# A peer layer in one core: tile 0's experts chosen ahead of the dense tiles, and sixteen instead of eleven row groups inside the first gates

## The reference, cut to what matters

```python
def peer(h, w_query, sub_keys, expert_down, expert_up):   # 512 tokens, 8 heads, 128 x 128 experts
    qry = (ht @ w_query).reshape(T, PEER_HEADS, 2, PEER_HALF_2)
    sub_scores = jnp.einsum('thpc,hpkc->thpk', qry, sub_keys)
    top_s, top_i = lax.top_k(sub_scores, K)                # K = 16, for each half of the key
    cand_s = top_s[:, :, 0, :, None] + top_s[:, :, 1, None, :]
    cand_id = top_i[:, :, 0, :, None] * N_KEYS + top_i[:, :, 1, None, :]
    best_s, best_c = lax.top_k(cand_s.reshape(T, PEER_HEADS, K * K), K)
    expert_id = jnp.take_along_axis(cand_id.reshape(...), best_c, axis=-1)
    gate = jax.nn.softmax(best_s, axis=-1)
    u = expert_down[ids]                                   # 128 rows of 1024 for each token
    act = jax.nn.gelu(jnp.einsum('pd,ped->pe', x, u)) * gate
    return jnp.einsum('pe,ped->pd', act, expert_up[ids])
```

## Time and profile before

| | us |
|---|---|
| median of three runs (lowest, highest) | 3564.9 (3564.6, 3565.7) |
| the profiled execution | 3564.92 |
| its span | 3563.0 |
| TensorE busy | 3195.5 (90%) |
| VectorE busy | 2433.8 (68%) |
| ScalarE busy | 1317.7 (37%) |
| gate loop from, to the first weighed block, first peer layer | 748.8, 886.1 |
| first weighed block, end of the last second product, first layer | 886.1, 1824.5 |
| the same in the second layer | 2615.6, 3554.9 |

### The profile page before, as it was taken

The page is one execution under the profiler, slowest core; times in us unless marked ns, Lnnn a source line. Parts: engine busy times, 40 slices in busy tenths (PEclk is TensorE's granted clock), DMA queues, the critical chain, the costliest instruction groups (busy, mean ns, idle before and its releaser), DMA issues. The chain is left out here.

```text
span 3563.0 us, 45086 instructions
## 1 busy us (share of the span) xinstructions
PE 3195.5 (90%) x16120; PEld 1998.7 (56%) x16120; DVE 2433.8 (68%) x5465; ACT 1317.7 (37%) x3292; POOL 1329.9 (37%) x1028
## 2 busy tenths in 40 slices
PE   6988889945999999999979998996589999999989
PEld 3443554534666666666534465454456666666654
DVE  1037752789897987877761234359989799788777
ACT  2122211134765655541011125112456556555300
POOL 0000000016565676766610000000556566676665
PEclk9999889967999999999989998998689999999999
DMA  3213213128999999999962110211689999999998
GB/s 119 81 61 138 99 65 130 44 76 313 345 405 349 402 398 405 409 409 409 409 251 71 53 65 13 105 49 48 245 311 386 381 374 391 405 409 409 409 409 346
DMA packets 271695, 908.11 MB, mean 255 GB/s; under 512 B 30536, under 2 KB 31192, under 8 KB 270960
## 3 DMA queue, kind: packets, MB, share of 16 engines
q0 software_dynamic: 147456, 536.94, 38.7%
q1 hardware_dynamic: 124016, 368.29, 27.4%
HBM read 900.90 MB, written 4.22 MB: 254 GB/s over the span
## 5 line engine op out<-in xcount | busy, mean ns | idle before, releaser
L679 PE MATMUL psum<-hT,mod 128*128 128x256 f32 x4096 | 986.8, 396 | 74.6 <-ACT hT L1094 41.5
L679 PEld LDWEIGHTS psum<-hT,mod 128*128 128x128 f32 x4096 | 793.4, 198 | 203.8 <-issue 96.0
L1104 ACT ACTIVATE levels<-key_numbers,hT 128x128 bf16<-128x128 f32 x1712 | 542.6, 388 | 367.4 <-PE psum L715 361.1
L1864 POOL DMA_INDIRECT w<-in_peer_u,tmp x172 | 234.9, 1366 | 895.7 <-DVEq L1551 789.3
L1693 DVE SCALAR_TENSOR_TENSOR tmp<-w,small,tmp 128x1024 f32<-128x1024 f32 x339 | 435.6, 1285 | 63.8 <-DMA w<-in_peer_up,tmp 27.0
L1673 DVE CUSTOM_DVE_ANT_0 w<-w,hn 128x1024 f32<-128x1024 f32 x342 | 407.8, 1222 | 65.5 <-DMA w<-in_peer_down,tmp 32.1
L1864 POOL DMA_INDIRECT big<-in_peer_down,tmp x86 | 119.0, 1383 | 769.1 <-DVEq L1551 711.7
L715 PEld LDWEIGHTS psum<-x,levels 128*128 128x128 bf16 x6144 | 226.8, 102 | 258.5 <-DVE levels L1613 128.3
L715 PE MATMUL psum<-x,levels 128*128 128x32 bf16 x6144 | 240.9, 196 | 141.2 <-DVE levels L1613 119.4
L689 PE MATMUL psum<-rows,big 128*128 128x512 f32 x800 | 358.6, 592 | 0.0
L1864 POOL DMA_INDIRECT w<-in_peer_down,tmp x170 | 233.0, 1370 | 114.4 <-DVE small L1673 71.4
(11 more groups left out here) (300 smaller groups left out, 4049.7 us busy)
## 6 DMA issues: line engine op xcount, KB each, us to landing
mod<-in_uT SPq DMA_DIRECT2D x256, 512.0 KB, 6.8
rows<-in_peer_v SPq DMA_DIRECT2D x64, 512.0 KB, 6.8
rows<-in_peer_up SPq DMA_DIRECT2D x64, 512.0 KB, 6.8
w<-in_w_in SPq DMA_DIRECT2D x14, 2048.0 KB, 7.8
w<-in_ada_w SPq DMA_DIRECT2D x12, 2048.0 KB, 7.9
srow<-in_peer_v SPq DMA_DIRECT2D x32, 512.0 KB, 7.0
tmp<-in_peer_v SPq DMA_DIRECT2D x32, 512.0 KB, 6.9
srow<-in_peer_up SPq DMA_DIRECT2D x32, 512.0 KB, 7.0
```

Source lines behind the costliest of these rows:

```text
L679: last = nc.tensor.matmul(ps[4 + e % 2][:, 0:ND], ub[e % UV][:, k, :], hT[:, k, ND:SEQ], start=k == 0, stop=k == KC - 1)
L1104: last = nc.scalar.activation(hits[n % HITS][:, j * P:(j + 1) * P], keyno, ACT.Abs, bias=nibT[:, n * BATCH + j:n * BATCH + j + 1])
L1864: nc.gpsimd.indirect_dma_start(ring[n % ROWS], None, table, bass.IndirectOffsetOnAxis(idx[:, c:c + 1], 0))\
```

## The change

Choosing: before the gate loop tile 0 goes first. Pairs 0 to 2 are chosen for tile 0, then tile 2, then tile 3; then come tile 0's numbers of six heads, its pair 3 and its last numbers and gates; then, tile after tile, pair 3, all numbers and the gates of tiles 2 and 3. In the gate loop no piece of a choice is left, and `first_pieces` with `EARLY_PIECES` is gone. Units: the loop runs sixteen, one in every fourth batch from batch 0 on; `UNITS` is made for the 112 that remain. On ScalarE `gate_exp(0)` moves from the loop to the head of `first_acts`.

```diff
-EARLY_PIECES = 3 * PAIR_PIECES
-FIRST_UNITS = 11
+FIRST_UNITS = 16
...
-def first_pieces(n):
-    return min(PIECES, EARLY_PIECES + n + 1)
...
 def first_units(n):
-    return max(0, min(FIRST_UNITS, (n - 16) // 4))
+    return 0 if n < 0 else min(FIRST_UNITS, n // 4 + 1)
...
             def first_acts(layer):
+                gate_exp(0)
                 block_gelu(layer, 0)
...
-                    if first_pieces(n - 2) <= EXP_PIECE < first_pieces(n - 1):
-                        gate_exp(0)
...
                     dve.wait_ge(sc_used, 16 * layer + 4 * (p + 1))
-                    for t in DENSE + (0,) if p < 2 else DENSE:
+                    for t in (0,) + DENSE if p < 3 else (0,):
                         for _ in head_experts(t, p):
                             pass
                     if p == 2:
-                        for t in DENSE:
-                            for _ in numbers(t, 0, EARLY_HEADS):
-                                pass
+                        for _ in numbers(0, 0, EARLY_HEADS):
+                            pass
+                for _ in last_numbers_and_gates(0):
+                    pass
                 for t in DENSE:
-                    for _ in last_numbers_and_gates(t):
+                    for _ in tile_experts(t, 3):
                         pass
-                for _ in head_experts(0, 2):
-                    pass
...
-                chooser = [tile_experts(0, EARLY_PIECES // PAIR_PIECES), tile_experts(1, 0)]
+                chooser = tile_experts(1, 0)
...
-                    for _ in range(first_pieces(n - 1), first_pieces(n)):
-                        next(chooser[0])
                     for u in range(first_units(n - 1), first_units(n)):
                         run_unit(layer, u)
```

More of the change, by code:

```diff
@@ L1643, in peer @@
                     for _ in range(pieces_due(e - 1), pieces_due(e)):
-                        next(chooser[1])
+                        next(chooser)
                     for n in range(units_due(e - 1), units_due(e)):
```

## The result

| | before | after |
|---|---|---|
| median of the runs on one chip, us (lowest, highest) | 3565.24 (3564.63, 3565.74) | **3592.06** (3590.55, 3594.18) |
| ratio, 95% interval | | 1.0075 (1.0062 to 1.0087) |
| span of the profiled execution | 3563.0 | 3591.3 |
| gate loop from, first layer | 748.8 | 777.7 |
| first weighed block, layers 1 and 2 | 886.1, 2615.6 | 910.0, 2655.5 |

The change makes the kernel 0.75% slower, 26.8 us; 3590 was forecast. I go through the same views as before. The slices of the page tell as little as the earlier trace rows: DMA is at 8 and 9 tenths in both layers.

A forecast was written before the change was run, and what follows sets the result against it. VectorE's work was taken to release the main phase, TensorE then to set its pace, rows its late stretch. A layer: 2 + 24.8 - 4.0 = 22.8 us later, less 10.3 back, 12.5; two layers 25, so 3590 us, range 3570 to 3610.

The forecast's parts named there:

- VectorE releases the main phase: Ahead of the main phase: work put on VectorE delays it one for one; start 22.8 us later in each layer.
- The picks' cover: Before the gate loop: VectorE loses work that hid turning and copying the dense picks; 2 us, bounds 0.7 and 4.
- The wait for the first rows: Start of the gate loop: VectorE's 4.0 us wait for the first gathered rows goes, as they land under the dense choice.
- the pace: Main phase up to block 60: TensorE alone sets 7.73 us a block pair, from (3091.63 - 2623.25) / 60.6.
- In the sum they are nothing: Tile 0's pieces, 25.3 us, moved ahead of the gate loop: it starts 25 us later and is 25 us shorter.
- What comes back: Main phase, stretch where rows set the pace: two units fewer, 5.1 us each by bytes, make it 10.3 us shorter.
- Only those 18.5 can be won: Main phase of 940 us: taking transfers out can win only TensorE's 18.5 us of waits from 3092 to 3500 us.
- the fourth case: Not slower, 0.15: transfers bound the whole main phase and hold TensorE's pace; five units give back 25.6 us a layer, 3559.
- The second: Nothing comes back, 0.13: GpSimd's issue and the ring of six bound the row stretch, not bytes; 3614 us.
- The third: Late stretch, 0.17: all 18.5 us of TensorE's waits come back, a smoother table keeping VectorE far enough ahead; 3574 us.
- The fifth: Gate loop, 0.05: its units wait for rows, as gathers share DMA with dense blocks; 5 to 8 us longer, 3603.
- The rule against the reading: Where TensorE is busy 50 of 50 us and DMA full, the waits tell which one bounds, not either share.

The follow-up runs named there:

- the units alone: The kernel before, old order of the choice, with sixteen instead of eleven units in the gate loop: 3600.32 us, ratio 1.0081.
- the order alone: The changed kernel's new order of the choice with eleven units, in their batches as before, against the kernel before: 3590.09 us, ratio 1.0063.
- the half rows: The changed kernel with gathers behind the first six of each ring fetching 512 of 1024 floats: 3561.46 us, ratio 0.9986 to the kernel before.
- a shifted table: The kernel before with its table of units shifted by up to five units at block 60, by nothing from block 105: 3545.52 us, ratio 0.9918.

## Why the prediction was right, and where its steps were not

**VectorE releases the main phase: right.** The first weighed block moved by 23.9 us in the first layer, for 22.8 in the sum; 0.8 of it was there at the first choice.

**Its terms.** The first gather was put at 721 us and came at 722.08. The loop start was put at 776 and came at 777.7. The picks' cover: 2 us taken, 2.3 measured in the first layer and 1.0 in the second, within 0.7 to 4. The cause was the one named: the product that stands ahead of the picks follows 19.8 us of idle time with 6.42 us. The wait for the first rows went. The loop takes 132.3 us for 137.3, that is 5.0 less; the sum had 24.8 - 25.3 - 4.0 = -4.5. With the cover as measured the sum is 24.8 + 2.3 - 4.0 = 23.1, and 23.1 were measured from the first choice on; in the second layer 22.0 (cover 1.0, wait for rows 3.8) and 21.9. In the pace, 60.6 isn't a count of blocks: 60 pairs lie between the two products, with 1.8 us of waits and the first blocks' larger share of gates; the 7.73 itself is what the chain shows from pair to pair.

**"In the sum they are nothing": right in this kernel, wrong as a reason.** Of the pieces I said that the loop gets shorter by their length. Taken out alone, they leave 12.5 us of idle time in the loop. The changed kernel shows none of it because five more units stand there, from batch 0 on. The split of the cost in the prediction (order 2 us, units 24.8) is thus only one of two ways to tell it: from the other side the order costs 10.9 and the units in it 12.2 more (24.8 less the 12.5 that they fill). The sum came out because both edits were made at once. For the units alone the rows would have given the time as well; for the order alone they missed by the 12.5 us of idle time, as my expectation did.

**What comes back: right.** 10.3 us a layer from two units; measured 6.7 and 11.6. The mean is 9.2; the single layers are 3.6 under and 1.3 over. That the rest above 913 us goes with the bytes of rows, and only in the late stretch, is shown by the half rows. That a unit is worth its 5.1 us there isn't: over the table the worth of one varies from 3 to 15.

**All that can be won: too small.** "Only those 18.5 can be won" took TensorE's waits as the reserve. The floor of 913 us says 25: the slow product behind each long wait belongs to it.

**The cases.** The pace stayed 7.73 us, as forecast, so the fourth case is out. The second (nothing comes back, late waits of 18) is out with waits of 11.9 and 10.1. The third, all waits back by a smoother table, isn't what this change does, but is what a shifted table does. The fifth, waits for rows in the loop, is out: there were none. The second layer's loop began 44.8 us later, of which 17.2 were the first layer's; the other 27.6 are near the 28.9 of the first, and I have no term missing there.

**The rule against the reading.** The Trainium skill ("Perfetto Trace Analysis", Identifying the Most-Contended Engine) takes the engine with the highest occupancy, and for DMA the HBM utilization in place of occupancy. Ahead of block 60 the half rows took a fifth of DMA's share (0.97 to 0.77) and a third of its rate (373 to 256 GB/s) away, and the time of that stretch didn't move; in the late stretch, at 1.01 and 401 GB/s in the changed kernel, bytes did cost time. The measurement decides: neither figure told the two stretches apart, TensorE's waits did.

## What to carry to other kernels

Work that fills an engine's gaps has a price that depends on what else fills them: cost two such edits together, and test each alone before you believe the terms. Where one stretch of a phase is bound by bytes and the next to it isn't, moving work over the border inside the phase pays (here 0.8% with three lines), while moving it ahead of the phase costs the engine that releases it. The reserve of a bound engine is its waits and the slow work behind the long ones.

## What the hardware showed unexpectedly

The share of DMA at 409 GB/s (1.03) stands with TensorE at 50 busy us of 50 in one kernel and 45.4 of 50 in another: a full transfer stretch may or may not hold its consumer. A first product of 16 matmuls took 3.54 us in the main phase and 3.69 behind waits of 1.0 to 1.8 us, both at a granted clock of 1.00; it took 5.38 behind a wait of 2.9 us (clock 0.68) and 6.42 behind one of 19.8 us (0.57).
